# Hybrid mLSTM and differential-attention block on one core: the split activation buffers y and hid placed 2432 bytes further on, with a gap between the halves of hid

## What is computed

```python
h = rms_norm(x, norm1_w)
proj = h @ w_in                       # mLSTM q,k,v,o and gates; attention q,k,v
y = concat(mlstm(proj), diff_attention(proj))
x = x + y @ w_out
h = rms_norm(x, norm2_w)
x = x + (silu(h @ w_gate) * (h @ w_up)) @ w_down
```

## Time and profile before

| | |
|---|---|
| median of 3 runs | 1150.81 us (1149.97 to 1150.9) |
| profiled execution: time | 1151.05 us |
| profiled execution: span, first to last instruction | 1149.3 us |
| TensorE busy with matmuls | 1130.5 us, 98% |
| VectorE, ScalarE busy | 52%, 47% |
| mean busy share of the DMA engines | 54% for the queue of the weights |
| granted TensorE clock, mean | 0.999 of full |

### The profile page before, as it was taken

One profiled execution on the slowest core, in us unless ns is written; L12 is line 12 of the kernel. 1 busy time (PEld: TensorE's weight loads), 2 busy tenths in 40 slices (PEclk: granted clock), 3 DMA queues, 4 the chain that ended last, 5 costly groups with the idle time before them and its releaser, 6 DMA issues.

```text
span 1149.3 us, 14440 instructions
## 1 busy us (share of the span) xinstructions
PE 1130.5 (98%) x5064; PEld 930.3 (81%) x5064; DVE 600.8 (52%) x685; ACT 537.8 (47%) x665; POOL 4.5 (0%) x20
## 2 busy tenths in 40 slices
PE   6999999899999999999999999999999999999998
PEld 5888887788888888888888888888888888888886
DVE  5576466564665655455454554554554544454443
ACT  7565476554554454444444444434444433333331
POOL 1000000000000000000000000000000000000000
PEclk9999999999999999999999999999999999999999
DMA  9555444554455556555555555555555555555554
GB/s 350 185 177 186 149 147 142 177 178 162 159 171 187 179 172 211 185 185 198 182 183 201 181 200 185 183 198 183 185 199 182 185 186 197 184 185 194 187 184 128
DMA packets 59651, 212.45 MB, mean 185 GB/s; under 512 B 6736, under 2 KB 6736, under 8 KB 59616
## 3 DMA queue, kind: packets, MB, share of 16 engines
q1 hardware_dynamic: 59408, 211.84, 54.0%
q10 hardware_dynamic: 144, 0.05, 0.0%
q0 software_dynamic: 64, 0.07, 0.0%
HBM read 209.83 MB, written 2.10 MB: 184 GB/s over the span
## 4 chain that ended last, share of the span: by engine, by line
PE 96%; DVE 2%; ACT 1%; issue 0%; DMA 0%; ACTq 0%
PE acc L378 27%; PE acc L381 27%; PE acc L380 27%; PE aux L381 4%; PE aux L378 4%; PE aux L380 4%; PE aux L392 2%; DVE w_lo L898 1%; DVE conv L1066 0%; DMA xt<-in_x_turned 0%; PE aux L442 0%; ACT w_hi L645 0%; DVE res L1208 0%; PE aux L494 0%; ACT conv L779 0%
## 5 line engine op out<-in xcount | busy, mean ns | idle before, releaser
L898 DVE TENSOR_TENSOR w_lo<-w_raw,w_hi 128x1024 fp32r<-128x1024 f32 x392 | 478.5, 1225 | 459.0 <-ACT w_hi L652 338.9
L378 PE MATMUL acc<-w_lo,act_hi 128*128 128x512 f32 x1088 | 429.5, 395 | 13.4 <-DVE w_lo L898 13.4
L652 ACT ACTIVATE w_hi<-w_raw 128x1024 fp32r<-128x1024 f32 x256 | 271.3, 1061 | 364.9 <-PE acc L381 227.2
L381 PE MATMUL acc<-w_hi,act_hi 128*128 128x512 f32 x1088 | 425.0, 391 | 0.0
L380 PE MATMUL acc<-w_hi,act_lo 128*128 128x512 f32 x1088 | 424.7, 390 | 0.0
L378 PEld LDWEIGHTS acc<-w_lo,act_hi 128*128 128x128 f32 x1088 | 205.0, 188 | 57.3 <-issue 10.8
L381 PEld LDWEIGHTS acc<-w_hi,act_hi 128*128 128x128 f32 x1088 | 205.1, 188 | 43.3
L380 PEld LDWEIGHTS acc<-w_hi,act_lo 128*128 128x128 f32 x1088 | 205.2, 189 | 41.5
L645 ACT ACTIVATE w_hi<-w_raw 128x1024 fp32r<-128x1024 f32 x136 | 141.9, 1057 | 81.2 <-PE acc L381 72.1
L378 PE MATMUL acc<-w_lo,hid_hi 128*128 128x512 f32 x176 | 69.5, 395 | 0.0
L378 PE MATMUL aux<-w_lo,hid_hi 128*128 128x512 f32 x176 | 69.5, 395 | 0.0
(11 more groups left out here) (191 smaller groups left out, 534.1 us busy)
## 6 DMA issues: line engine op xcount, KB each, us to landing
w_raw<-in_weights SPq DMA_DIRECT2D x392, 512.0 KB, 3.3
res<-in_x SPq DMA_DIRECT2D x4, 512.0 KB, 9.7
out<-res SPq DMA_DIRECT2D x8, 256.0 KB, 3.8
xt<-in_x_turned SPq DMA_DIRECT2D x3, 512.0 KB, 8.1
xt<-in_x_turned SPq DMA_DIRECT2D x2, 256.0 KB, 4.8
w_if<-in_gate_w POOLq DMA_DIRECT2D x1, 64.0 KB, 5.9
par<-in_params ACTq DMA_DIRECT2D x1, 47.0 KB, 4.3
bias_if<-in_gate_bias POOLq DMA_DIRECT2D x1, 0.0 KB, 5.5
```

Of the source, the lines that this page charges most:

```text
L378: pe.matmul(bank[:], hi[:, k, tok], w_lo[:, slot, cols], start=first and kk == 0, stop=False)
L381: mm = pe.matmul(bank[:], hi[:, k, tok], w_hi[:, slot, cols], start=False, stop=last and kk == len(kts) - 1)
L652: act.activation(w_hi[:, c % SPLIT, :], w_raw[:, c % RAW, :], ACT.Copy).then_inc(hi_done, 1)
L898: dve.tensor_tensor(w_lo[:, slot, :], w_raw[:, slot, :], w_hi[:, slot, :].bitcast(F32), ALU.subtract).then_inc(lo_done, 1)
```

## The change

The unused buffer ahead of `y_hi` grows by 608 numbers (2432 bytes) per partition, and a new unused one of 4096 bytes stands between `hid_hi` and `hid_lo`. All other buffers of the scopes `mix` and `ff` move on with them, by 2432 bytes. No instruction is added, removed or reordered.

```diff
-        sb("line_pad", [24])
+        sb("line_pad", [24 + 608])
...
         hid_hi = sb("hid_hi", [KF, SEQ], F32R, ff)
+        sb("hid_pad", [1024], F32, ff)
         hid_lo = sb("hid_lo", [KF, SEQ], F32R, ff)
```

## The result

The changed kernel takes 1142.65 us (median of 4 runs, 1142.02 to 1143.05) against 1150.8 us before (4 runs, 1149.97 to 1150.9). The ratio is 0.9931, 95% interval 0.9918 to 0.9943: 8.15 us less, outside of noise. The prediction was 1142.7.

A forecast was written before the change was run, and what follows sets the result against it. TensorE, busy 98% of the span, was taken to bound the kernel. -2.15 us on y and -5.91 on hid, all else 0, gave -8.1 us and 1142.7 us, with a range of 1141.3 to 1151.3.

The forecast's parts named there:

- The bound: Whole kernel: TensorE is busy 98% of the span, so time changes only through one matmul's cost or its few waits.
- The size: Output and down projections: y's 384 and hid's 1056 matmuls take act's step, 5.6 ns less each, -8.1 us.
- The cover: Down projection: ScalarE and VectorE still feed weights in time when a 12-matmul chunk lasts 2.72 us instead of 2.79; 0.
- The mixer's buffers: Mixer: its own buffers move by 2432 bytes, affecting about 80 short matmuls; -0.45 to +0.45 us, taken as 0.
- hid_pad: Feed-forward scope: this buffer is never touched, and changed write times to hid and y cause no wait near w_lo's; 0.
- What makes a place good: Stationary y and hid lie 256 past a multiple of 512, act and weights 128; this offset costs 5.6 ns a matmul.
- Rival 1, height: Output and down projections: the step depends on how high the stationary operand lies; time unchanged, 1150.8 within 0.4; chance 0.30.
- The evidence from the gate matmuls: Gate matmuls on w_if_parts, at 184608: 119.4 ns for 256 columns, 12.7 over 106.7, held against height and offset alike.
- Rival 2, half: Output and down projections: offset is one of two causes, or helps one stage or term; about half of 8.1, 1146.8; chance 0.08.
- Rival 3, a worse meeting: Output and down projections: sharing the weights' offset above 128 KB is worse, 8.6 ns a matmul, +12.4 us, 1163; chance 0.06.

The follow-up runs named there:

- the first quarter step: Kernel before with line_pad larger by 64 bytes and a gap of 56 numbers heading hid's scope (y 64, hid 32 past a multiple of 256): 1150.3 us, one run.
- the third quarter step: Kernel before with line_pad larger by 160 bytes and a gap of 16 numbers heading hid's scope (y 160, hid 224 past a multiple of 256): 1152.34 us.
- the 16 bytes: Kernel before with y and hid sliced from larger buffers behind gaps, 144 and 112 past a multiple of 256, weights at 128: 1145.77 us, one run.

## Why the prediction was right

- **The bound.** TensorE's steps set the three stages, as the first part has it: 8.0 of the 8.3 us by which the span fell came out of the step, and none came back as waiting.
- **The size.** The sum took act's step for y and hid, 384 and 1056 times 5.6 ns: 2.15 and 5.91 us. Measured 2.0 and 6.0. The forecast span was 1141.2, the span is 1141.0.
- **The cover.** 0 for ScalarE and VectorE at 2.72 us a chunk: right, TensorE is busy 240.50 of 240.50 us in the last stage.
- **The mixer's buffers.** 0 within 0.45 us. The 0.3 us by which y's first start moved is within that and within the scatter: it stands at 316.0 to 317.6 in the eleven kernels that leave the weights' place alone. Part of this scatter is the clock. Seven of their twelve traces, before and after among them, have a stretch of 3.4 us around 222 us in which the granted clock was 0.50, which is 1.2 GHz, and y starts at 316.7 to 317.6 in them; the five without it have y at 316.0 to 316.6. TensorE was busy for 1.17 of the 3 us before 221.0 in the kernel before. The kernel before, and the first quarter step:

```profile
221.20:224.60 3.40, 3.40 (x10) 2.61 (x9) 3.29 (x3) 1.97 (x3) 0.00 (x0) 0.50 0.72 228
221.20:224.60 3.40, 2.89 (x13) 2.38 (x14) 2.52 (x3) 3.19 (x4) 0.00 (x0) 1.00 0.43 152
```

- **hid_pad.** 0: right, and the larger line_pad alone, without this gap, shows it.
- **What makes a place good.** The prediction named the offset over a multiple of 512, "which the change takes away". The kind of cause was right, two things in it were not exact: the period is 256 bytes, and it is the distance to the moving operand that is repeated, not a place. The list of its reasons contained the second, since act's blocks lie at 128 "as do the weights", but the sum did not need it: giving y and hid act's offset gives them act's distance to the weights as well, so the sum comes out by either reading. The prediction could not tell the two apart, and to that extent its number was safer than its reason.
- **Rival 1, height** (0.30) and with it the rule of the Trainium skill: out. y and hid are still the highest, with the shortest step, and act got the long one without being moved. The Trainium skill, "SBUF — State Buffer", section "Who interferes with whom", gives TensorE ports of its own and says it never waits on anyone. No run here shows another engine in its way. "TensorE: Matmul & The Clock Gate" of the Trainium skill, in "Step-by-step: what each phase is for", has it that loading the next block does not steal read bandwidth from the running matmul. The runs don't show what goes on inside, but they don't let the two operands pass as independent: hid's step is 226.7 ns at one distance and 234.2 at another, with the same instructions. The measurement decides.
- **The evidence from the gate matmuls** that was held against both offset and height was misread. Their stationary blocks begin at steps of 64 bytes from 184608, which is 32 over a multiple of 256, and act, now the moving operand, lies at 128: the distances are -96, -32, +32 and +96 in turn, none of them 0. The two kernels whose gaps shift w_if_parts to 192 over a multiple of 256, the third quarter step and the 16 bytes, give these matmuls +64, 128, -64 and 0 instead. By the starts in the traces their 31 steps take 3.64 us there and 3.69 in the kernel before, 117.3 against 119.1 ns each. So the 119.4 of the prediction was a long step too, the price of placement shows on 256 columns as well, and the 12.7 ns were no argument against offset. Before, last start; third quarter step, first and last start:

```profile
44.90 0.28 PE L403 MATMUL aux<-act_lo,w_if_parts 128*128 128x256 f32 x1
...
41.83 0.28 PE L403 MATMUL aux<-act_hi,w_if_parts 128*128 128x256 f32 x1
...
45.46 0.28 PE L404 MATMUL aux<-act_lo,w_if_parts 128*128 128x256 f32 x1
```

- **Rival 2, half:** steps of 228 to 231 ns exist at some distances, but not at the one that was chosen.
- **Rival 3, a worse meeting** of blocks at the same offset: the sign is the other way. Equal offsets are the best case. Unequal ones can be worse than what the kernel had, but by little: 234.2 ns at +96 is 1.8 over 232.4, not the 8.6 that were feared.

## What to carry to other kernels

Where matmuls of one shape follow one another without a wait and still take two different steps, sort the steps by buffer before looking for a cause in time or in other engines; 5.6 ns on 1440 matmuls were 0.7% here. For blocks like these (float32r, 128 x 128 stationary, 512 columns moving), let the stationary and the moving operand begin at the same byte over a multiple of 256, in all loops that use them, and look where a buffer of odd size ahead of them has pushed the ones behind; one gap of 128 bytes did it. The price goes with every matmul, so a gap that mends one pair and breaks another must be counted over both, as moving the weights shows with 18 us more than moving y and hid alone.

## What had not been expected of the hardware

- In this kernel a matmul of 512 columns whose next stationary block is loaded beside it steps by 226.7 ns if both operands begin at the same byte over a multiple of 256, and by 228 to 234 ns if they don't. Which of ten distances is taken matters, and not evenly: -64 bytes gives 228.9, +64 gives 233.4, +96 gives 234.2.
- The long step is not one duration but a pattern. At a distance of 128 bytes hid's starts were 0.23 to 0.25 us apart; by the starts in the trace six steps in seven take 228 to 233 ns and every seventh 240 or 241. At 0 they are even, 226 or 227 ns but for some ten of over a thousand:

```profile
999.71 0.39 PE L379 MATMUL aux<-w_lo,hid_hi 128*128 128x512 f32 x1
999.94 0.39 PE L381 MATMUL aux<-w_hi,hid_lo 128*128 128x512 f32 x1
1000.17 0.39 PE L382 MATMUL aux<-w_hi,hid_hi 128*128 128x512 f32 x1
1000.39 0.39 PE L379 MATMUL acc<-w_lo,hid_hi 128*128 128x512 f32 x1
1000.62 0.39 PE L381 MATMUL acc<-w_hi,hid_lo 128*128 128x512 f32 x1
```

- The best step seen, 226.7 ns, is still 13.4 over 512 cycles of the full clock (512 / 2.4 GHz = 213.3 ns). Ten distances gave none shorter on the mean. What the 13.4 ns are was not tried, and neither was whether distances of 8 bytes or less are free.
